# A two-layer hybrid decoder step on one core: a new split of a background job's work between two stages of layer 0

## The chip, the cores and the metric

The kernel runs on one core of a Trainium2 chip. The metric is the device time of one execution in microseconds (us), median of several runs.

## The reference, cut to what matters

One inference step for a prompt group (512 tokens) and a sample group (8 tokens, one for each of 8 batches, with 4096 cached positions each). Both groups use the same weights. Per layer:

```
def layer_forward(x, ...):
    xn = rms_norm(x, norm1_g)
    z, xbc, dt, q, k, v, iq, ik, iw, gate_a, gate_b = split(xn @ w_in)
    y_a = mamba2_branch(...)              # causal conv over xbc, then the state-space scan
    y_b = dsa_prompt(...) or dsa_sample(...)
    x = x + (sigmoid(gate_a) * (y_a @ w_branch_a) + sigmoid(gate_b) * (y_b @ w_branch_b)) @ w_out
    return x + peer_ffn(rms_norm(x, norm2_g))

def dsa_sample(...):                      # the part that is moved here belongs to this
    score = indexer_scores(iq, concat([ik_past, ik]), iw)      # 4097 scores per batch
    _, idx = top_k(score, 256)
    return sparse_attend(q, gathered cache_k rows, gathered cache_v rows)

def peer_ffn(xn):                         # 8 heads x 16 experts for each token
    s = einsum(xn @ wq, keys); sv, si = top_k(s, 16)           # routing
    act = gelu(einsum(u[eidx], xn)); return einsum(gate * act, v[eidx])
```

## The kernel before

The prompt's 512 tokens are cut into two halves of two 128-token tiles, `Half(0)` and `Half(1)`. For each layer and each half the kernel runs through a fixed row of stages: norm1, xbc (projection and causal convolution, `project_conv`), tokproj, ssd, ssmout, qkv, attn0, attn1, mix, norm2, pscore, route. A stage (`stage`, L127) is a block in which each engine has its own in-order stream; at its end all five engines meet at a barrier (L133), so a stage lasts as long as its last engine.

Beside these stages up to three background jobs run. Job "S" (`Sample`) does the decode mixer of the 8 sample tokens; job "U" does the expert dot products (gathered rows of `peer_u` times the token), job "V" the expert sums. A job is a set of generators, one for each engine, that yield a due time in the job's own units before each piece. `PLAN_SAMPLE` (and `PLAN_DOTS`, `PLAN_SUMS`) say how many of the job's units belong to each stage; within a stage, `Beside.to` issues, at points of the stage's own work (`go(part)`), the pieces whose share of the stage's units has come. The order within each engine's stream is thus fixed when the program is built; nothing is scheduled at run time.

Job "S" has 405 units: the state-space part 0 to 80, qkv 80 to 110, the index scores 110 to 165, the top-k 165 to 295, the sparse attention 303 to 405 (`SAMPLE_PARTS`). It begins with the mix stage of half 0 and ends with the tokproj stage of half 1. The end of the top-k is the packing of the keys' positions (the "key packing"): the 129 score columns of two halves of the batches are worked through in 14 chunks, 6 of 19 columns and one of 15 for each half (`sample_topk_vector`, L1874 to L1884). VectorE makes two one-hot tables and a payload in four instructions for each chunk (L1878, L1880, L1882, L1883); TensorE then does one small fp32 matmul a column (L1802, two records each in the trace), waiting with `hot` for VectorE's chunk, and VectorE waits with `taken` so that it is at most two chunks ahead. Then VectorE copies two results (L1888, `packed`), SyncE issues 16 small DMAs to `ssel` and waits for them (L1901 to L1903), and the sparse attention begins: `s_qz` (L1914 to L1918) on VectorE, transposes of `ssel` and the spreading of the new key (L1985, L1990) on TensorE, row numbers (L1924 to L1927), 16 key and value gathers of four batches in a row on GpSimd's queue (L1974), and for each batch a chain that goes back and forth: patch (L1934, VectorE), transposes (L2005, TensorE), copy `s_kT` (L1937, VectorE), scores (L2015, TensorE), scale and maximum (L1941 to L1944, VectorE), exponential (ScalarE), transposes (L2020, TensorE), copy (L1947, VectorE), values (L2025, TensorE), scale (L1953, VectorE).

In the xbc stage of half 1 there are 24 blocks f of 128 channels. TensorE does 16 matmul records for a block (L533), ScalarE evacuates it (L553 to L556), VectorE convolves it in four instructions (L581, L583), ScalarE applies SiLU. Three PSUM banks and two buffers of `raw` and `conv` let TensorE run some blocks ahead of VectorE. Job "U" runs beside it in layer 0: 49 expert rows, each a gather on GpSimd's queue (L2619) into a ring of five rows and one instruction on VectorE (L2655), which frees the row for the next gather. In layer 0 neither "U" nor "V" runs beside the route stage of half 0, since there are no experts yet.

Where a piece falls in a stage follows from the units. A chunk u is due on VectorE at 165 + 130 x (0.63 + 0.025 x (u + 0.2)) and on TensorE at 165 + 130 x (0.63 + 0.025 x (u + 1)).

Of the kernel before, what the change touches and what calls it, by code (L numbers as in the profile page):

```python
# [346 lines left out]
def turn_vectors(nc, G, l, rows, taps, fetch):  # L347

    early = G.ahead.goals()
    with stage(nc, G, "vectors", "vectors") as (block, sem):  # L350
        loaded, goal = (sem("loaded"), 16 * 11) if fetch else (G.ahead.sems[0], early[0])

        if fetch:
            @block.sync
            def _(sp):
                for dst, src in vector_loads(G, l, rows, taps):
                    sp.dma_start(dst, src).then_inc(sem("loaded"), 16)
                sp.wait_ge(sem("loaded"), 16 * 11)

        @block.tensor  # L360
        def _(pe):
            pe.wait_ge(loaded, goal)
            pe.transpose(G.bank[2][:, 0:32], rows[:], G.ident[0:32, 0:32])
            for f in range(FT):
                last = pe.transpose(G.bank[f // 16][:, 32 * (f % 16):32 * (f % 16) + BC_ROWS],
                                    taps[:, f * P:(f + 1) * P], G.ident[0:BC_ROWS, 0:BC_ROWS])
            last.then_inc(sem("turned"), 1)

        @block.vector
        def _(dve):  # L370
            dve.wait_ge(sem("turned"), 1)
            done = Own(dve, sem("copied"))
            done.mark(dve.tensor_copy(G.gcol[:], G.bank[2][:, 0:32]))
            for h in range(2):
                n = min(16, FT - 16 * h)
                src = G.bank[h][:, 0:32 * n].rearrange("p (f c) -> p f c", c=32)[:, :, 0:BC_ROWS]
                done.mark(dve.tensor_copy(G.taps[:, 16 * h:16 * h + n, :], src))

            dve.memset(G.hT[:], 0.0)
            dve.wait_ge(sem("exp"), 1)  # L380
            done(dve.tensor_scalar(G.na[:], G.na[:], -1.0, None, ALU.mult))

        @block.scalar
        def _(act):
            act.wait_ge(loaded, goal)
            act.activation(G.na[:], G.na[:], ACT.Exp).then_inc(sem("exp"), 1)
# [104 lines left out]
def conv_weights(G, l, u):  # L491

    return G.w_in[l, :, C_XBC + 2 * P * u:C_XBC + 2 * P * (u + 1)].rearrange("(k p) c -> p k c", p=P)
# [145 lines left out]
def token_weights(G, l, chunk):  # L639

    return G.w_in[l, :, chunk[0]:chunk[0] + chunk[2]].rearrange("(k p) c -> p k c", p=P)
# [358 lines left out]
def tail_rows(G, S, t):  # L1000

    rows = slice(t * P, t * P + P)
    return (S.tail[:], G.tokm[rows, T_Q:T_Q + QKV]), (S.cs[:], G.rope[rows])
# [375 lines left out]
SAMPLE_TIME = 405.0  # L1379
# [747 lines left out]
SAMPLE = {"POOL": sample_pool, "SP": sample_sync, "DVE": sample_vector, "ACT": sample_scalar, "PE": sample_tensor}  # L2127
# [4 lines left out]
def gate_weights(G, l):  # L2132

    return G.w_in[l, :, C_GA:C_GA + 2 * P].rearrange("(k p) c -> p k c", p=P)
# [664 lines left out]
def hybrid_step(nc, ins, outs, rope):  # L2799
    G = Names()  # L2800
# [19 lines left out]
    with ExitStack() as top:  # L2820
        def sb(name, shape, dt=F32, stack=top):
            return stack.enter_context(nc.sbuf_tensor(name, shape, dt, allow_name_mangling=True))
# [55 lines left out]
        for l in range(DEPTH):  # L2878
            for H in (Half(0), Half(1)):
                with ExitStack() as mixer:  # L2880
                    def keep(name, shape):
                        return mixer.enter_context(nc.sbuf_tensor(name, shape, F32, side="right", allow_name_mangling=True))
                    with ExitStack() as ssm:
                        if not H.late and l == 0:
                            with nc.sbuf_tensor("gain_rows", [32, P], F32, allow_name_mangling=True) as rows, \
                                    nc.sbuf_tensor("tap_rows", [BC_ROWS, CD], F32, allow_name_mangling=True) as taps:
                                turn_vectors(nc, G, l, rows, taps, True)
                        with nc.sbuf_tensor("wx", [P, 4, KD, 2 * P], F32, side="right", allow_name_mangling=True) as wx:
                            wt = wx[:].rearrange("p (s h) k c -> p s (h k c)", h=2).rearrange("p s (k c) -> p s k c", c=BANK)
                            norm_tokens(nc, G, H, 0, "norm1", True, [[(wx[:, u], conv_weights(G, l, u))] for u in range(2)])  # L2890
                            G.xcT = sb("xcT", [P, FT, H.n_in], stack=ssm)
                            project_conv(nc, G, H, l, wx, [(wt[:, 0, :, 0:chunks[0][2]], token_weights(G, l, chunks[0]))], "xbc")
                            project_tokens(nc, G, H, l, chunks, wt, "tokproj")
                        if H.late:
                            G.beside.finish("S")
                            G.stale.append(range(SAMPLE_SEM0, SAMPLE_SEM0 + SAMPLE_SEMS))
                            store_conv_state(nc, G, l, "convst")
                        G.yaT = keep("yaT", [P, XT, H.n_out])
                        if True:
                            S = Names()  # L2900
                            at = Region(nc, f"m{l}{H.i}_", G.region)
                            S.y, S.xs, S.z = at("y", [P, DI]), at("xs", [P, DI]), at("ztile", [P, DI])
                            S.xdd, S.ytmp = at("xdd", [P, 2, DI // NG]), at("ytmp", [P, DI // NG])
                            A = Names()
                            at = Region(nc, f"a{l}{H.i}_", G.region)
                            A.qT, A.iqT, A.roped = at("qT", [P, AH // 2, P]), at("iqT", [P, IH // 2, P]), at("roped", [P, ROPED + 1, HD])
                            at.top = at.base + 2 * 4 * DI
                            A.tail, A.cs = at("tail", [P, QKV]), at("cs", [P, 2, HD // 2])
                            for j, t in enumerate(H.tiles):
                                ssd_chunk(nc, G, S, l, t, j, "ssd")  # L2910
                                ssm_output(nc, G, S, l, P, t * P, j * P, H.late and j == 1, tail_rows(G, A, H.tiles[0]) if j == 1 else (), "ssmout")
                    G.ybT = keep("ybT", [P, KD, H.n_out])
                    wm = keep("wm0", [P, KD, 2 * P])
                    if True:
                        S = A
                        for j, t in enumerate(H.tiles):
                            rows = slice(t * P, (t + 1) * P)
                            attention_inputs(nc, G, S, l, P, t, t * P, j == 0,
                                             (G.k_prompt[l, 0, rows].rearrange("t h d -> t (h d)"),
                                              G.v_prompt[l, 0, rows].rearrange("t h d -> t (h d)"), G.idx_k_prompt[l, 0, rows]), "qkv")  # L2920
                            attention_prompt(nc, G, S, l, t, j, j == 0, [(wm[:], gate_weights(G, l))] if j == 1 else [], f"attn{j}")
                    if not H.late:
                        G.beside.begin("S", Job(SAMPLE, Sample(nc, G, l, G.region), SAMPLE_TIME, PLAN_SAMPLE, ORDER_SAMPLE))
                    G.mixT = keep("mixT", [P, KD, H.n_out])
                    mix_branches(nc, G, H, l, wm, "mix")
                G.g2src = G.norm2_g[l]
                with ExitStack() as peer:
# [5 lines left out]
                    S = Names()  # L2933
# [58 lines left out]
ORDER_FIRST = ("norm1", "xbc", "tokproj", "ssd", "ssmout", "ssd", "ssmout", "qkv", "attn0", "qkv", "attn1", "mix", "norm2", "pscore", "route")  # L2992
ORDER = (("route2", "vectors") + ORDER_FIRST, ORDER_FIRST[:3] + ("convst",) + ORDER_FIRST[3:] + ("route2",))
ORDER_SAMPLE = ("mix", "norm2", "pscore", "route", "norm1", "xbc", "tokproj")
PLAN_SAMPLE = {"mix": 165, "norm2": 4, "pscore": 74, "route": 56, "norm1": 4, "xbc": 32, "tokproj": 70}
PLAN_DOTS = ({"route2": 22, "vectors": 4, "norm1": 0, "xbc": 37, "tokproj": 90, "ssd": 10, "ssmout": 3, "attn0": 14, "attn1": 26, "mix": 54,
              "last": 247, "last_rush": 0.88},
             {"norm1": 0, "xbc": 50, "tokproj": 85, "convst": 5, "ssd": 10, "ssmout": 2, "attn0": 22, "attn1": 24, "mix": 51})
# [46 lines left out]
```

## Time and profile before

| | |
|---|---|
| median of 3 runs | 5554.57 us (5540.15 to 5554.66) |
| profiled execution, its own time | 5553.32 us |
| its span | 5551.6 us |
| TensorE / VectorE / GpSimd / ScalarE busy | 78% / 64% / 45% / 22% of the span |
| mean granted TensorE clock | 0.869 of full speed |

The span is what the profiler saw of the program; 1.7 us of the execution's own time lie around it. No engine is busy throughout; which of them sets the time has to be read stage by stage. The stages spoken of here were located by the barrier's instructions (L133): pscore 822.7 to 896.2, route 896.2 to 1048.1, norm1 1048.1 to 1061.9, xbc 1061.9 to 1204.7, tokproj 1204.7 to 1401.5 us from the span's start.

### The profile page before, as it was taken

How to read it: one execution, taken by the hardware profiler on the slowest of the kernel's cores; microseconds unless marked ns; L12 is line 12 of the kernel's file. 1: busy time of each engine (PE TensorE's matmuls, PEld its weight loads, DVE VectorE, ACT ScalarE, POOL GpSimd, SP SyncE). 2: the span in 40 equal slices, each digit the busy share in tenths (PEclk: the TensorE clock that was granted, in tenths of full speed). 3: DMA queues.
4: the chain of work that ended last, by engine and by line, in shares of the span. 5: the costliest groups of instructions: out<-in, count | busy, mean ns of one | idle time of the engine just before them, and what ended most of it. 6: DMA issues, size and time to landing. Idle time of an engine off the chain costs nothing. (4 is left out here: it accounts for less than half of the span.)

```text
span 5551.6 us, 50287 instructions
## 1 busy us (share of the span) xinstructions
PE 4303.1 (78%) x15868; PEld 2639.8 (48%) x15868; DVE 3538.2 (64%) x7830; ACT 1214.3 (22%) x3036; POOL 2477.7 (45%) x2215
## 2 busy tenths in 40 slices
PE   7955886668678989589677786968778798767777
PEld 6334775543334766263344575553344476223333
DVE  4055648866678546686676868966668754844444
ACT  2042311121332112120432311121233211111111
POOL 0000010166455544546565333456655553577776
PEclk9975997689788999899898898988888899888888
DMA  4310641489788987789889876689878797799999
GB/s 142 117 62 29 236 151 43 150 282 346 261 274 270 328 291 271 276 307 375 289 299 319 322 247 221 204 295 341 300 261 278 269 360 264 258 371 409 409 409 360
DMA packets 583999, 1484.68 MB, mean 267 GB/s; under 512 B 60616, under 2 KB 251688, under 8 KB 581320
## 3 DMA queue, kind: packets, MB, share of 16 engines
q0 software_dynamic: 307200, 1115.82, 55.6%
q1 hardware_dynamic: 261272, 331.39, 18.0%
q10 hardware_dynamic: 15264, 34.26, 1.6%
q8 instruction: 129, 2.11, 0.2%
q14 instruction: 134, 1.10, 0.1%
HBM read 1435.37 MB, written 45.93 MB: 267 GB/s over the span
## 5 line engine op out<-in xcount | busy, mean ns | idle before, releaser
L2747 PE MATMUL duo<-vring,diag 128*128 128x512 f32 (+1 forms) x2976 | 1516.1, 660 | 397.0 <-DMA vring<-in_peer_v,eidx 169.0
L2619 POOL DMA_INDIRECT uring<-in_peer_u,eidx x981 | 1147.4, 1170 | 1117.6 <-DVE uring L2655 661.4
L2700 POOL DMA_INDIRECT vring<-in_peer_v,eidx x1024 | 1127.5, 1101 | 1035.9 <-PE duo L2747 471.8
L2747 PEld LDWEIGHTS duo<-vring,diag 128*128 128x128 f32 (+1 forms) x2976 | 593.9, 209 | 1199.9 <-issue 955.0
L2655 DVE SCALAR_TENSOR_TENSOR uring<-uring,xr 128x1024 f32<-128x1024 f32 x795 | 958.6, 1221 | 200.9 <-DMA uring<-in_peer_u,eidx 177.0
L689 PE MATMUL duo<-wx,xT 128*128 128x512 f32 (+3 forms) x1440 | 607.7, 580 | 32.2 <-PEq L133 32.1
L2780 DVE SCALAR_TENSOR_TENSOR x_tok<-vring,wt,x_tok 128x1024 f32<-128x1024 f32 x296 | 385.3, 1302 | 94.2 <-DMA vring<-in_peer_v,eidx 67.8
L2728 ACT ACTIVATE diag<-ident,wt 128x128 f32<-128x128 f32 x728 | 269.6, 395 | 742.0 <-PE duo L2747 677.9
L689 PEld LDWEIGHTS duo<-wx,xT 128*128 128x128 f32 (+1 forms) x1440 | 240.1, 178 | 387.1 <-issue 386.0
L2655 DVE SCALAR_TENSOR_TENSOR uring<-uring,duo 128x1024 f32<-128x1024 f32 x201 | 245.4, 1221 | 264.5 <-DMA uring<-in_peer_u,eidx 263.9
L533 PE MATMUL duo<-xT,wx 128*128 128x264 f32 (+1 forms) x1536 | 357.5, 397 | 36.6 <-ACT newcols L556 30.3
L533 PEld LDWEIGHTS duo<-xT,wx 128*128 128x128 f32 x1536 | 302.9, 198 | 91.5 <-issue 35.9
L1673 POOL IOTA s_rowi<- 128x8 int32 x2 | 0.3, 148 | 692.3 <-DVEq L1372 692.3
L2215 PE MATMUL duo<-xT,wm 128*128 128x256 f32 (+1 forms) x1024 | 251.2, 405 | 18.2 <-PEq L133 8.8
L2215 PE MATMUL duo<-yaT,wm 128*128 128x256 f32 (+1 forms) x1024 | 250.6, 406 | 16.8 <-DMA wm<-in_w_branch_a 16.5
L2321 PE MATMUL duo<-xT,wq 128*128 128x256 f32 (+1 forms) x1024 | 244.4, 394 | 0.0
L2215 PEld LDWEIGHTS duo<-xT,wm 128*128 128x128 f32 x1024 | 204.9, 202 | 62.2 <-issue 16.3
L2215 PEld LDWEIGHTS duo<-yaT,wm 128*128 128x128 f32 x1024 | 205.7, 203 | 57.9 <-DMA wm<-in_w_branch_a 19.1
L2321 PEld LDWEIGHTS duo<-xT,wq 128*128 128x128 f32 x1024 | 197.7, 198 | 29.3
L1802 PE MATMUL duo<-s_pay,s_hota 128*64 128x32 f32 x1032 | 91.7, 260 | 80.3 <-DVEq L1884 80.3
L1168 PE MATMUL duo<-kT,a_qT 64*128 64x128 f32 (+3 forms) x256 | 103.7, 535 | 58.8 <-DVE s L1264 47.7
L583 DVE SCALAR_TENSOR_TENSOR conv<-raw,taps,conv 128x256 f32<-128x256 f32 x288 | 139.6, 485 | 10.2
(471 smaller groups left out, 5262.4 us busy)
## 6 DMA issues: line engine op xcount, KB each, us to landing
wx<-in_w_in SPq DMA_DIRECT2D x32, 2048.0 KB
wx<-in_w_in SPq DMA_DIRECT2D x48, 1024.0 KB, 8.2
wm<-in_w_in SPq DMA_DIRECT2D x32, 1024.0 KB, 11.4
wm<-in_w_branch_a SPq DMA_DIRECT2D x32, 1024.0 KB, 11.2
wq<-in_peer_wq SPq DMA_DIRECT2D x32, 1024.0 KB, 7.8
tokm<-tout ACTq DMA_DIRECT2D x64, 256.0 KB
eb<-decays SPq DMA_DIRECT2D x32, 512.0 KB, 4.4
s_h<-in_state_ssm SPq DMA_DIRECT2D x32, 512.0 KB, 9.2
```

The lines of the kernel that those rows point to most:

```text
L533: mm = pe.matmul(G.bank[f % NB][:, 0:n], w[:, u % NW, k, (f % 2) * P:(f % 2 + 1) * P], G.xT[:, k, 0:n], start=(k == 0), stop=(k == KD - 1))
L583: last = dve.scalar_tensor_tensor(a, win, tap, a, ALU.mult, ALU.add)
L689: mm = pe.matmul(G.bank[u % 3][0:n, 0:width], G.xT[:, k, j * P:j * P + n], w[:, s, k, 0:width], start=(k == 0), stop=(k == KD - 1))
L1168: mm = pe.matmul(duo[0][:, q, 0:W], S.qT[lo:lo + HD, c, :], G.kT[lo:lo + HD, g // 2, 0:W], start=True, stop=True)
L2215: mm = pe.matmul(tile_bank(c, part, f)[:, 0:n], w[u % NW][:, k, f * P:(f + 1) * P], acts[name][:, k0 + k, 0:n], start=(k0 + k == 0), stop= ...
L2321: mm = pe.matmul(b[:, 0:n], w[:, u % NW, k, (f % 2) * P:(f % 2 + 1) * P], G.xT[:, k, 0:n], start=(k == 0), stop=(k == KD - 1))
L2619: pool.indirect_dma_start(out=E.rings.urows[K % E.ur], out_offset=None, in_=table, in_offset=bass.IndirectOffsetOnAxis(ap=E.tiles[q][3][:, ...
L2655: dve.scalar_tensor_tensor(row, row, 1.0, xr, ALU.mult, ALU.mult, accum_out=G.pre[:, q % 2, j:j + 1]).then_inc(G.dotted, 1)
L2700: pool.indirect_dma_start(out=E.rings.vrows[K % E.vr], out_offset=None, in_=table, in_offset=bass.IndirectOffsetOnAxis(ap=E.tiles[q][3][:, ...
L2728: act.activation(G.diag[:, K % DR, 0:m], sel, ACT.Copy, scale=G.wt[:, q % 2, j:j + 1]).then_inc(G.diagged, 1)
L2747: mm = pe.matmul(G.bank[6 + c][0:m, :], G.diag[:, R % DR, 0:m], E.rings.vrows[K % E.vr][:, c * BANK:(c + 1) * BANK], start=first, stop=las ...
L2780: dve.scalar_tensor_tensor(x, E.rings.vrows[K % E.vr], G.wt[:, q % 2, j:j + 1], x, ALU.mult, ALU.add).then_inc(G.folded, 1)
```

## The change

`PLAN_SAMPLE` becomes a pair, one plan for each layer. Layer 1 keeps the numbers. In layer 0 the route stage of half 0 gets 28 units in place of 56, and the xbc stage of half 1 gets 60 in place of 32; the sum stays 405. The stages' bounds in the job's units move from route 243 to 299, norm1 to 303, xbc to 335 to route 243 to 271, norm1 to 275, xbc to 335.

```
-    G.beside.begin("S", Job(SAMPLE, Sample(nc, G, l, G.region), SAMPLE_TIME, PLAN_SAMPLE, ORDER_SAMPLE))
+    G.beside.begin("S", Job(SAMPLE, Sample(nc, G, l, G.region), SAMPLE_TIME, PLAN_SAMPLE[l], ORDER_SAMPLE))
...
-PLAN_SAMPLE = {"mix": 165, "norm2": 4, "pscore": 74, "route": 56, "norm1": 4, "xbc": 32, "tokproj": 70}
+PLAN_SAMPLE = ({"mix": 165, "norm2": 4, "pscore": 74, "route": 28, "norm1": 4, "xbc": 60, "tokproj": 70},
+               {"mix": 165, "norm2": 4, "pscore": 74, "route": 56, "norm1": 4, "xbc": 32, "tokproj": 70})
```

## Rows read from the trace of the kernel before

**Rows 1.** The page: span, and busy time of each engine.
```profile
span 5551.6 us, 50287 instructions
...
PE 4303.1 (78%) x15868; PEld 2639.8 (48%) x15868; DVE 3538.2 (64%) x7830; ACT 1214.3 (22%) x3036; POOL 2477.7 (45%) x2215
```

**Rows 2.** Windows, route: us, busy PE, PEld, DVE, ACT, POOL, PEclk, DMA share, GB/s.
```profile
896.20:1045.90 149.70, 57.96 (x516) 56.08 (x516) 141.38 (x546) 1.90 (x3) 0.00 (x0) 0.50 0.00 1
1045.90:1048.10 2.20, 0.00 (x0) 0.00 (x0) 0.00 (x0) 0.00 (x0) 0.00 (x0) 0.50 0.02 1
```

**Rows 3.** Windows of the xbc stage, cut where VectorE's stalls begin and end.
```profile
1061.90:1071.70 9.80, 7.40 (x20) 6.02 (x21) 0.02 (x1) 0.54 (x3) 0.00 (x0) 0.56 1.00 323
1071.70:1113.90 42.20, 42.20 (x198) 37.14 (x197) 41.06 (x86) 14.37 (x47) 25.67 (x21) 1.00 0.94 336
1113.90:1131.70 17.80, 8.97 (x42) 7.56 (x40) 1.50 (x5) 0.93 (x4) 13.53 (x15) 0.82 0.89 278
...
1154.30:1204.70 50.40, 37.01 (x138) 27.76 (x138) 38.23 (x80) 15.53 (x39) 23.63 (x20) 0.80 0.68 233
```

**Rows 4.** Timeline of VectorE, route: start us, us, instruction. A full chunk, a narrow one, `packed`.
```profile
957.61 1.42 DVE L1878 TENSOR_TENSOR s_hota<-s_digf,colf 128x1216 f32<-128x1216 f32 x1
...
960.52 2.29 DVE L2450 TENSOR_TENSOR hot<-ab,iota 128x2048 f32<-128x2048 f32 x1
...
1026.86 1.16 DVE L1878 TENSOR_TENSOR s_hota<-s_digf,colf 128x960 f32<-128x960 f32 x1
...
1029.30 2.29 DVE L2450 TENSOR_TENSOR hot<-ab,iota 128x2048 f32<-128x2048 f32 x1
...
1036.27 0.28 DVE L1888 COPY s_packed<-duo 64x32 f32<-64x32 f32 x2
```

**Rows 5.** Timeline of SyncE's queue from the end of route.
```profile
1036.58 10.06 SPq L1901 DMA_DIRECT2D ssel<-s_packed  x16
```

**Rows 6.** Timeline of TensorE: a full chunk's matmuls in layer 0, and in layer 1.
```profile
960.48 4.26 PE L1802 MATMUL duo<-s_pay,s_hota 128*64 128x32 f32 x38 [5.61 <-DVEq L1884]
```
```profile
3483.70 2.40 PE L1802 MATMUL duo<-s_pay,s_hota 128*64 128x32 f32 x38
```

**Rows 7.** Timeline of TensorE and VectorE, norm1 and the start of xbc.
```profile
1059.53 2.05 PE L1990 MATMUL duo<-newkv,ident 8*128 8x256 f32 x4
1064.30 2.08 PE L533 MATMUL duo<-xT,wx 128*128 128x256 f32 x4 [2.72 <-DMA wx<-in_w_in]
```
```profile
1059.28 0.19 DVE L439 TENSOR_TENSOR xT<-duo,gcol 128x32 f32<-128x32 f32 x1 [0.16 <-PE duo L452]
1059.47 0.27 DVE L1914 MEMSET s_qz<- 128x256 f32 x1
1059.78 0.82 DVE L1918 COPY s_qz<-qTs 64x32 f32<-64x32 f32 x4
```

**Rows 8.** Timeline of VectorE, xbc: two successive blocks' convolutions, the stall behind the gathers.
```profile
1075.80 0.35 DVE L581 TENSOR_SCALAR conv<-raw,taps 128x256 f32<-128x256 f32 x1
...
1079.92 0.35 DVE L581 TENSOR_SCALAR conv<-raw,taps 128x256 f32<-128x256 f32 x1
```
```profile
1131.68 1.23 DVE L2655 SCALAR_TENSOR_TENSOR uring<-uring,xr 128x1024 f32<-128x1024 f32 x1 [16.19 <-DMA uring<-in_peer_u,eidx]
```

**Rows 9.** Timeline of TensorE, xbc, while the first batch of the sparse attention runs.
```profile
1155.09 1.12 PE L2005 MATMUL duo<-ident,s_kv 128*128 128x128 f32 x4 [11.38 <-DVE s_kv L1934]
...
1158.13 5.95 PE L533 MATMUL duo<-xT,wx 128*128 128x256 f32 x16
1167.32 1.89 PE L2015 MATMUL duo<-s_kT,s_qz 128*16 128x256 f32 x4 [3.24 <-DVEq L1938]
...
1181.10 0.30 PE L2020 MATMUL duo<-ident,s_s 16*128 16x16 f32 x2 [2.94 <-ACT s_s L2042]
```

**Rows 10.** Timeline of VectorE, xbc: convolutions that waited for TensorE's block.
```profile
1164.69 0.35 DVE L581 TENSOR_SCALAR conv<-raw,taps 128x256 f32<-128x256 f32 x1 [3.20 <-ACT newcols L556]
...
1175.32 0.35 DVE L581 TENSOR_SCALAR conv<-raw,taps 128x256 f32<-128x256 f32 x1 [5.58 <-ACT newcols L556]
```

## The prediction

> **What bounds the kernel now.** I read the page first, for whether one engine fills the span: none does, TensorE is busy for 78% and VectorE for 64% [rows 1], so an edit has to be priced in its own stages. Then I laid windows over route, norm1 and xbc, where work goes out and comes in. In route VectorE has work for 141.4 of the 149.7 us until its last instruction, and the rest lies between its instructions; for 2.2 us more all engines are idle [rows 2]. That stage is one serial VectorE stream and then a wait for SyncE: 16 small DMAs are issued from 1036.58 for 10.06 us, the last issued at 1046.6, and the barrier opens only when they have landed [rows 5]. In xbc nothing is computed on VectorE for 9.8 us, until the first block is projected; then comes a stretch of 42.2 us in which VectorE works for 41.1; then 17.8 us in which it does 1.5 us of work; and at the end 50.4 us with 38.2 busy [rows 3]. The reader is to see that VectorE's order paces this stage, and that its idle time lies in three definite places. The timelines say which: the long stall waits for a gathered expert row [rows 8], and the late ones for blocks that TensorE brings late because it goes back and forth with VectorE over the sparse attention [rows 9, 10].
>
> **What leaves route.** With 28 units for route a chunk is due on VectorE at fraction (165 + 130 x (0.63 + 0.025 x (u + 0.2)) - 243) / 28. Chunk 7 comes to 0.975 and chunk 8 to 1.09. So chunks 8 to 13 leave, one for norm1 and five for xbc. A full chunk holds VectorE from 957.61 to the next instruction at 960.52, 2.91 us; a narrow one from 1026.86 to 1029.30, 2.44 us [rows 4]. Chunk 13 is narrow: 5 x 2.91 + 2.44 = 17.0 us. The `packed` copies leave too: 0.3 us, with the gap behind them 0.4 [rows 4]. Nothing else covers these, as TensorE's matmuls for them (4.26 us each [rows 6]) run beside VectorE's other work. And the 16 DMAs go to xbc, with them the 2.2 us tail [rows 2]. Together -19.5 us (17.4 + 2.1, as the barrier itself stays). This is the firm part.
>
> **norm1.** It gets VectorE's chunk 8 (2.9 us) and TensorE's chunk 7 (38 records at the cold rate, 4.1 us), both behind tile 0. It loses `s_qz` (1.3 us on VectorE) and the spreading (2.05 us and the transposes before it on TensorE) [rows 7]. The three tiles' transposes are behind chunk 7, so VectorE's last `xT` ends some 4.1 us later, at 1063.6 instead of 1059.5, and the barrier comes at about 1063.7 instead of 1061.9: +1.8. But the first matmul of xbc waited for its weights until 1064.30 [rows 7], at a DMA share of 1.00 [rows 3], so the weights hide this. Another effect has the other sign: TensorE then works nearly without a pause from its first transposes into xbc. If that leaves its granted clock at 2.4 GHz, the first 16 records are quicker by up to 16 x (0.427 - 0.216) = 3.4 us (rates: 42.2 us over 198 records at full clock are 0.213 [rows 3], with the gaps 0.216; cold it is twice that). I take 0, with bounds of -3.4 and +1.8.
>
> **xbc, VectorE's own work.** Five chunks, 4 x 2.91 + 2.44 = 14.1; `packed` 0.4; `s_qz` 1.3: 15.8 us. The cover would be idle time of VectorE. Chunks 9 to 13 are due at 0.03, 0.08, 0.14, 0.19 and 0.25, and `packed` at 0.30, so they stand behind blocks 0, 2, 3, 4, 5 and 7. The first 9.8 us of idle time are over by then (chunk 9 stands behind block 0's convolution in VectorE's stream), and behind them comes the stretch that is 97% busy, two rows and a convolution in 4.12 us per block [rows 3, 8]. So the 15.8 us lie on the path in full. Queued behind each chunk are two expert rows and the next convolution, and behind that ScalarE's evacuation and TensorE.
>
> **xbc, TensorE's part.** The six chunks 8 to 13 of matmuls are 5 x 38 + 30 = 220 records, 23.5 us at layer 0's rate (4.1 to 4.26 for 38) and 13.9 at layer 1's (2.40) [rows 6]. A block takes 3.4 us of TensorE against VectorE's 4.12, so some of it fits: per chunk VectorE gains 2.9 and TensorE 2.4. But TensorE's order now has it wait for VectorE's chunk behind block f before block f + 2, where it ran four to five blocks ahead. A VectorE wait of about 2 us should come of that at two places. I take +4, bounds 0 (all hidden) and 13.9.
>
> **xbc, the gathers.** GpSimd issues the 16 key and value gathers in a row, which starves the ring of five rows: 16.19 us [rows 8]. They move from fraction 0.32 to 0.64 of the stage, still one row of 16, still ahead of the same ring. The stall moves and stays: +1, bounds 0 and +2. For SyncE's queue: `ssel` holds it for 10.06 us plus the landing, between the weight loads for u = 7 and u = 8. TensorE wants u = 8 at block 16, VectorE is then past block 11, and the stall behind the gathers comes later. I price it at nothing; without that cover it is 11 us.
>
> **xbc, the back and forth.** This is where I expect the loss. The attention's first batch keeps its order, but the blocks between its steps halve, since 32 units became 60. As blocks behind which each step stands (V for VectorE, T for TensorE):
> before: patch V15, transposes T16, `s_kT` V17, scores T17, scale V18, exponential 19, transposes T19, copy V20, values T21, scale V21;
> after: V19, T19, V20, T20, V21, 21, T21, V22, T22, V22.
> Before, TensorE had done a block more than VectorE when it waited, so VectorE had a convolution to do meanwhile. After, TensorE can't begin block f + 1 until VectorE is done with f and the step; VectorE has only two rows, 2.3 us, to fill with.
> From patch to the next late convolution: TensorE's transposes at 1155.09 to 1164.69, 9.6 us [rows 9, 10], less 2.3: 7.3 idle (before 3.20). `s_kT`, scores from 1167.32 to the convolution at 1175.32, 8.0, with the hand-over before it 8.1, less 2.3: 5.8 (before 5.58); if TensorE is still at 2.4 GHz, 16 x 0.213 + 0.9 + 0.6 less 2.3, 2.6. The scale step: the exponential kept TensorE waiting for 2.94 us [rows 9], of which I count 1.9; 16 records 3.4, evacuation and the rest 1.0, less 2.3: 4.0, and 3.4 more cold. The copy: 1.0 + 3.4 + 0.7 less 2.3: 2.8, and 3.2 more cold. Sum 16.7 to 26.5. Before, the last stretch had 50.4 - 38.2 = 12.2 idle [rows 3]. So +4.5 to +14.3; I take +10, as waits of 3.24 and 11.38 us in rows 9 were followed by cold matmuls and these would be as long.
>
> The Trainium skill ("TensorE: Matmul & The Clock Gate", section "Loop structure matters more than you think") holds that copying results out by VectorE between matmuls does not break the array's warmth, while a long wait does. By it alone the cold parts drop out, the back and forth costs +4.5 and the whole +6. The trace disagrees for a wait of 3.24 us: the row behind it runs 1.89 us for four records.
>
> **Sum.** -19.5 + 0 + 15.8 + 4 + 1 + 10 = +11.3 us. Bounds: -19.5 - 3.4 + 15.8 + 0 + 0 + 4.5 = -2.6, and -19.5 + 1.8 + 15.8 + 13.9 + 2 + 14.3 = +28.3. The profiled execution took 5553.3 (span 5551.6 and 1.7 around it), 1.3 below the median of 5554.6; the change is added to the median: 5565.9. Tokproj has the same pieces in the same order and begins at a barrier, so I carry nothing over.
>
> **Rivals.** First, xbc absorbs it: 5535.1. Its VectorE is idle for some 40 us [rows 3], more than the 15.8 that come. For it: only if chunks ran in that idle time would they be free. Against: they are due in the first third, where idle is 1.1 of 42.2 us. It decides once the stage grows by less than 2.8 us (19.5 less 0.3%, 16.7). With part of it, the result is a gain too. Chance 0.12.
> Second, only VectorE's own work counts, and TensorE keeps its lead: -19.5 + 15.8 = -3.7, 5550.9. Against it: the table of blocks. It ends within 0.3%; I count it with "same".
> Third, the coupling is near its upper bound, TensorE cold through it, perhaps with u = 8 late: +20 to +28, 5580. For it: TensorE waits at every step and has 4.26 us of matmuls for a chunk when cold. Chance 0.33 for all that lies above +16.7.
> That the change does nothing can't be: chunks do change stages.
>
> **Numbers.** 0.3%, 16.7 us, is about what a measurement of this kernel can tell from no change. My forecast of +11 with its neighbours from -16.7 to +16.7, the second rival in it: 0.55. The likeliest one's own range is 5552 to 5583. For 8 in 10 the range takes in the low bound and part of the first rival: 5545 to 5584.
>
> **What would show it.** Route 132 to 133 us, and no idle tail before its barrier. Norm1 about 15.5, and xbc's first matmul near 16.2 us after norm1's start. xbc 170 to 177 in place of 142.8; six chunks' L1802 in it; the 16 us stall once, behind block 17; several waits of 3 to 7 us for `newcols` behind blocks 19 to 22. The prediction is wrong if xbc grows by under 20 us (the coupling or the chunks hide) or by over 36, or if tokproj changes by more than 3.

## The result, and the profile after

The changed kernel takes 5558.4 us (median of 18 runs, 5546.1 to 5568.9), the kernel before 5546.3 us on the same chip (18 runs). The ratio is 1.0024, with a 95% interval of 1.0014 to 1.0033: slower by 13.3 us, 7.8 to 18.3. That is inside the 0.3% that was named as the least a measurement can tell, and these runs did tell it. The forecast was +11.3 us, with 0.55 for "within 0.3%", and 5558.4 lies in the range of 5545 to 5584. The forecast was added to a median of 5554.6 for the kernel before; on this chip that kernel is 8.3 us quicker, so the difference is what to compare: +13.3 against +11.3.

The profiled execution of the changed kernel took 5551.8 us, with this head of its page (the lines that answer to [rows 1]):

```profile
span 5550.0 us, 50279 instructions
...
PE 4298.2 (77%) x15868; PEld 2627.9 (47%) x15868; DVE 3539.8 (64%) x7830; ACT 1213.6 (22%) x3036; POOL 2477.3 (45%) x2215
```

Its span is 1.6 us shorter than the one before, although the medians say 12 us longer. Single executions of either kernel scatter by some 10 us either way, so two spans can't be subtracted here. Lengths of stages can, once one knows how much a stage scatters. For that the kernel before was profiled a second time. Layer 0's stages in us, from the barriers in the traces:

```
                 pscore  route  norm1    xbc  tokproj
before             73.5  151.9   13.8  142.8    196.8
before, again      72.6  151.9   13.8  141.0    190.8
changed            73.3  132.1   16.0  171.4    189.3
difference         -0.2  -19.8   +2.2  +28.6     -7.5
```

(The difference is changed less before.) Route and norm1 repeat to 0.1 us, xbc to 2, tokproj only to 6. So most of tokproj's -7.5 can't be put down to the change: the second profile of the unchanged kernel shows 6.0 of it. An effect of 1 to 3 us isn't excluded: over all profiles of this document tokproj took 190.8 to 196.8 us where the attention keeps its old places in xbc, and 189.3 to 192.5 where it has the new ones. The prediction had named "tokproj changes by more than 3" as a sign of being wrong; the number is met, but a stage that moves by 6 on its own can't serve as such a sign. Route, norm1 and xbc give -19.8 + 2.2 + 28.6 = +11.0 us, inside the measured interval.

Windows over those stages of the changed kernel (us, then busy us and instructions of PE, PEld, DVE, ACT, POOL, then PEclk, DMA share, GB/s):

```profile
895.30:1027.15 131.85, 28.99 (x258) 28.05 (x258) 125.16 (x520) 1.82 (x3) 0.00 (x0) 0.50 0.00 0
...
1027.40:1043.40 16.00, 9.01 (x62) 8.19 (x62) 6.09 (x13) 8.05 (x11) 4.72 (x5) 0.50 0.94 344
1043.40:1050.50 7.10, 6.71 (x28) 5.31 (x28) 0.00 (x0) 0.54 (x3) 0.00 (x0) 0.63 0.98 314
1050.50:1098.00 47.50, 44.53 (x330) 38.28 (x329) 41.90 (x77) 7.94 (x29) 18.98 (x14) 0.89 0.63 205
...
1147.80:1165.70 17.90, 0.00 (x0) 0.00 (x0) 0.03 (x2) 0.00 (x0) 13.64 (x15) 0.59 0.68 230
...
1173.40:1214.80 41.40, 26.14 (x90) 18.49 (x90) 22.18 (x46) 10.31 (x24) 15.81 (x12) 0.83 0.40 136
```

Route lost its 2.2 us tail: VectorE works until 0.25 us before the barrier. The stretch without VectorE at the start of xbc is 7.1 us, not the 9.8 of [rows 3]. The stall with nothing on TensorE and little on VectorE is still 17.9 us long, later in the stage. And the last 41.4 us have only 22.2 busy on VectorE; before, the last 50.4 had 38.2.

What VectorE waited for in the whole xbc stage (us in total, times, longest), first in the kernel before, then in the changed one:

```profile
DVE conv L581 <- ACT newcols L556: 20.9, 4, 11.1
DVE uring L2655 <- DMA uring<-in_peer_u,eidx: 17.0, 2, 16.2
```
```profile
DVE conv L581 <- ACT newcols L556: 30.7, 10, 7.4
DVE uring L2655 <- DMA uring<-in_peer_u,eidx: 18.4, 2, 17.9
```

Waits for the block (`newcols`) rose from 4 to 10 and from 20.9 to 30.7 us; waits for gathered rows rose by 1.4 us only. VectorE's timeline says which ten they are; here are eight of them, and the row behind the gathers:

```profile
1050.51 0.35 DVE L581 TENSOR_SCALAR conv<-raw,taps 128x256 f32<-128x256 f32 x1 [7.37 <-ACT newcols L556]
...
1063.01 0.35 DVE L581 TENSOR_SCALAR conv<-raw,taps 128x256 f32<-128x256 f32 x1 [1.27 <-ACT newcols L556]
...
1097.63 0.35 DVE L581 TENSOR_SCALAR conv<-raw,taps 128x256 f32<-128x256 f32 x1 [1.52 <-ACT newcols L556]
...
1122.13 0.35 DVE L581 TENSOR_SCALAR conv<-raw,taps 128x256 f32<-128x256 f32 x1 [1.88 <-ACT newcols L556]
...
1165.71 1.22 DVE L2655 SCALAR_TENSOR_TENSOR uring<-uring,xr 128x1024 f32<-128x1024 f32 x1 [17.88 <-DMA uring<-in_peer_u,eidx]
...
1183.83 0.35 DVE L581 TENSOR_SCALAR conv<-raw,taps 128x256 f32<-128x256 f32 x1 [7.43 <-ACT newcols L556]
...
1191.76 0.35 DVE L581 TENSOR_SCALAR conv<-raw,taps 128x256 f32<-128x256 f32 x1 [2.88 <-ACT newcols L556]
...
1201.49 0.35 DVE L581 TENSOR_SCALAR conv<-raw,taps 128x256 f32<-128x256 f32 x1 [4.60 <-ACT newcols L556]
...
1208.86 0.35 DVE L581 TENSOR_SCALAR conv<-raw,taps 128x256 f32<-128x256 f32 x1 [2.50 <-ACT newcols L556]
```

They fall into four kinds. The first is the start of the stage. Four short ones (1.27, 1.52 and two not shown of 0.48 and 0.76, 4.0 us together) stand where a packing chunk's matmuls sit before TensorE's next block. One of 1.88 us at 1122 stands alone, behind the step in which TensorE transposes `ssel`. The last four, 7.43 + 2.88 + 4.60 + 2.50 = 17.4 us, stand at the steps of the sparse attention, each behind work that TensorE did for it. TensorE's timeline for these steps and for the wait at 1122 (in brackets what it waited for). "Cold" stands for a granted clock of 0.50, the 1.2 GHz level, and "warm" for 1.00, the 2.4 GHz level:

```profile
1113.12 0.41 PE L1985 MATMUL duo<-ident,ssel 8*128 8x8 f32 x4 [2.28 <-SPq L1372]
1113.39 1.94 PE L1990 MATMUL duo<-newkv,ident 8*128 8x256 f32 x4
...
1174.29 1.09 PE L2005 MATMUL duo<-ident,s_kv 128*128 128x128 f32 x4 [28.64 <-DVE s_kv L1934]
...
1177.31 5.91 PE L533 MATMUL duo<-xT,wx 128*128 128x256 f32 x16
1186.46 1.04 PE L2015 MATMUL duo<-s_kT,s_qz 128*16 128x256 f32 x4 [3.24 <-DVEq L1938]
...
1195.30 0.32 PE L2020 MATMUL duo<-ident,s_s 16*128 16x16 f32 x2 [4.15 <-ACT s_s L2042]
1195.55 5.33 PE L533 MATMUL duo<-xT,wx 128*128 128x256 f32 x16
1203.57 1.04 PE L2025 MATMUL duo<-s_kv,s_pT 128*16 128x256 f32 x4 [2.68 <-DVE s_pT L1947]
1204.53 3.72 PE L533 MATMUL duo<-xT,wx 128*128 128x256 f32 x16
```

The back and forth can be read straight off: TensorE waits for VectorE's step, does the step's matmuls, projects one block of 16 records, and only then VectorE's convolution can run. The row at 1113.12 is the wait that I had priced at nothing. `ssel` is ready only when SyncE's 16 small DMAs have landed, and TensorE stands still for it; what that cost VectorE is weighed further down. SyncE's queue of the changed kernel shows the issue that precedes it, 10.1 us long:

```profile
1099.77 10.10 SPq L1901 DMA_DIRECT2D ssel<-s_packed  x16
...
1113.14 1.01 SPq L515 DMA_DIRECT2D wx<-in_w_in  x2
```

### The profile page after: what moved, and what is told of

The parts are those of the page before. It is cut to its first block and busy times, and to the rows that moved or that the text cites. A ratio compares the mean times of both kernels' runs of the same rounds, so it can differ in the third digit from the quotient of the medians.

```text
span 5550.0 us, 50279 instructions
## 1 busy us (share of the span) xinstructions
PE 4298.2 (77%) x15868; PEld 2627.9 (47%) x15868; DVE 3539.8 (64%) x7830; ACT 1213.6 (22%) x3036; POOL 2477.3 (45%) x2215
## 3 DMA queue, kind: packets, MB, share of 16 engines
q8 instruction: 129, 2.11, 0.2%
## 5 line engine op out<-in xcount | busy, mean ns | idle before, releaser
L2655 DVE SCALAR_TENSOR_TENSOR uring<-uring,xr 128x1024 f32<-128x1024 f32 x795 | 959.1, 1221 | 206.9 <-DMA uring<-in_peer_u,eidx 181.6
L2655 DVE SCALAR_TENSOR_TENSOR uring<-uring,duo 128x1024 f32<-128x1024 f32 x201 | 245.4, 1221 | 265.0 <-DMA uring<-in_peer_u,eidx 264.5
L533 PE MATMUL duo<-xT,wx 128*128 128x264 f32 (+1 forms) x1536 | 365.1, 402 | 20.1 <-ACT newcols L556 16.5
L2215 PE MATMUL duo<-yaT,wm 128*128 128x256 f32 (+1 forms) x1024 | 245.6, 400 | 14.6 <-DMA wm<-in_w_branch_a 14.4
L2215 PEld LDWEIGHTS duo<-xT,wm 128*128 128x128 f32 x1024 | 203.7, 201 | 62.3 <-issue 16.9
L2215 PEld LDWEIGHTS duo<-yaT,wm 128*128 128x128 f32 x1024 | 202.2, 199 | 54.2 <-DMA wm<-in_w_branch_a 16.9
L2321 PEld LDWEIGHTS duo<-xT,wq 128*128 128x128 f32 x1024 | 196.8, 197 | 28.9
## 6 DMA issues: line engine op xcount, KB each, us to landing
wm<-in_w_in SPq DMA_DIRECT2D x32, 1024.0 KB, 11.3
```

Source lines behind the costliest of these rows:

```text
L533: mm = pe.matmul(G.bank[f % NB][:, 0:n], w[:, u % NW, k, (f % 2) * P:(f % 2 + 1) * P], G.xT[:, k, 0:n], start=(k == 0), stop=(k == KD - 1))
L2215: mm = pe.matmul(tile_bank(c, part, f)[:, 0:n], w[u % NW][:, k, f * P:(f + 1) * P], acts[name][:, k0 + k, 0:n], start=(k0 + k == 0), stop= ...
L2321: mm = pe.matmul(b[:, 0:n], w[:, u % NW, k, (f % 2) * P:(f % 2 + 1) * P], G.xT[:, k, 0:n], start=(k == 0), stop=(k == KD - 1))
L2655: dve.scalar_tensor_tensor(row, row, 1.0, xr, ALU.mult, ALU.mult, accum_out=G.pre[:, q % 2, j:j + 1]).then_inc(G.dotted, 1)
```

## The experiments

The two theories at the start. Mine: xbc pays for VectorE's own work in full, and then for an attention in which TensorE no longer runs ahead of VectorE, because its steps are spread over half as many blocks each. The rival: the chunks alone cost (their work, their matmuls, the place of the stall), and the attention's new spacing costs nothing. One experiment moves the attention alone, one the chunks alone. Line numbers of the experiments' kernels are shifted where lines were added (L2655 is L2657 or L2670).

**The kernel before, once more** (`before_again`), unchanged.

> The kernel before, unchanged, for one more profile: how much its stages vary from execution to execution, above all tokproj of half 1 in layer 0, which took 196.8 us in the first profile and 189.3 in the changed kernel's. If that stage's length is chance, this profile has it anywhere from 188 to 198 us, while route (151.9) and xbc (142.8) repeat within 1 us. If the shorter tokproj belongs to the change, this profile shows 196 to 198 again.

It took 5547.6 us. The table above has its stages: route and norm1 equal, xbc 1.8 us shorter (more than the 1 us that I had allowed), tokproj 6.0 us shorter.

**The attention alone** (`attend_only`): the kernel before and its plan, but layer 0's steps that were due between 303 and 335 units are due between 317.9 and 335, where the changed kernel has them. The chunks stay in route.

```diff
+MOVE = ((303.0, 303.0 + 32.0 * 28 / 60), (335.0, 335.0))
...
+def at_moved(program):
+    def steps(eng, J):
+        for t in program(eng, J):
+            yield moved(t) if J.l == 0 else t
+    return steps
...
```

The function `moved`, left out here, is linear between the points of `MOVE`; `at_moved` wraps every engine's part of job "S".

> The kernel before with its plan, and in layer 0 only the sparse attention's pieces at the places of the stage that the change gives them (due times 303 to 335 squeezed into 317.9 to 335); the key packing stays beside routing. My theory, that the back and forth loses TensorE's lead: route stays at 151.9 us, norm1 gets some 0.5 us shorter, xbc grows by the 1.3 us of s_qz and by 5 to 14 us of waits for blocks, 149 to 157 us in place of 142.8; in all 5 to 13 us slower, 1.001 to 1.0023. The rival, that only VectorE's own work counts: xbc 144 us, time unchanged. The stall behind the gathers stays at 16 us and moves to block 17.

Ratio 1.0028 (1.0014 to 1.0042), so +15.5 us. Norm1 took 11.6 us (-2.2), xbc 159.7 (+16.9); together +14.7. VectorE's waits in its xbc, and the four late convolutions:

```profile
DVE conv L581 <- ACT newcols L556: 33.1, 5, 11.7
DVE uring L2670 <- DMA uring<-in_peer_u,eidx: 18.3, 4, 16.6
```
```profile
1177.47 0.35 DVE L581 TENSOR_SCALAR conv<-raw,taps 128x256 f32<-128x256 f32 x1 [7.83 <-ACT newcols L556]
...
1188.28 0.35 DVE L581 TENSOR_SCALAR conv<-raw,taps 128x256 f32<-128x256 f32 x1 [5.76 <-ACT newcols L556]
...
1198.07 0.35 DVE L581 TENSOR_SCALAR conv<-raw,taps 128x256 f32<-128x256 f32 x1 [4.65 <-ACT newcols L556]
...
1206.85 0.35 DVE L581 TENSOR_SCALAR conv<-raw,taps 128x256 f32<-128x256 f32 x1 [3.17 <-ACT newcols L556]
```

The late ones sum to 21.4 us, against 9.85 in the kernel before (3.20 and 5.58 [rows 10] and one of 1.07). So with not a single chunk moved, the respacing of the attention alone makes the kernel slower by about as much as the whole change does (1.0028 and 1.0024, with intervals that overlap), and 11.6 of the 14.7 us are in these waits. The rival, which gave 0 here, is refuted; my own 149 to 157 for xbc was too low, by 3.

The ten profiles of this document bear it out. The waits of VectorE for a block in the attention's part of xbc sum to 7.3 to 9.9 us in the six in which the attention stands at about its old places, and to 17.3 to 21.4 us in the four in which it stands at the new ones.

**The chunks alone** (`chunks_only`): the changed kernel, with layer 0's attention steps pulled back to about the blocks that they stood behind before.

```diff
+MOVE = ((303.0, 303.0), (313.2, 306.8), (323.4, 313.25), (335.0, 335.0))
```

The functions around it are those of `attend_only`.

> The changed kernel, but with the sparse attention's first batches at the places of the xbc stage that they had before (patch at 0.64 of the stage in place of 0.81; the gathers at 0.53, as they have to come behind the packing). My theory: route 132 us as in the changed kernel, xbc shorter than the changed kernel's 171.4 by 5 to 12 us, 159 to 166 us, as the waits behind blocks 19 to 22 fall from 17 to 6 to 12 us; against the kernel before -2 to +6 us in all, ratio 0.9995 to 1.001. The rival (only VectorE's own work and the packing's matmuls cost, not the spacing of the attention): xbc stays at 170 to 172 us and the ratio at 1.0024.

Ratio 0.9992 (0.9978 to 1.0007): no difference that can be told. Route (132.2) and norm1 (16.0) are as in the changed kernel; xbc 159.2, 12.2 us less than it. VectorE's waits:

```profile
DVE conv L581 <- ACT newcols L556: 20.9, 7, 7.5
DVE uring L2670 <- DMA uring<-in_peer_u,eidx: 14.5, 1, 14.5
DVE s_kv L1934 <- DMA s_kv<-in_cache_v,s_coli: 1.5, 1, 1.5
```

Against the changed kernel that is 9.8 less for `newcols`, 3.9 less for gathered rows and 1.5 more for `s_kv`: the 12.2 us, to the tenth. The chunks by themselves cost xbc 16.4 us and earn 19.7 - 2.2 in route and norm1: 1 us is left over, less than these profiles can tell. VectorE's busy time in xbc is 102.1 us in the kernel before and 117.0 here, its idle time 40.7 and 42.1: the work that came found no cover. Other changes cancel in that idle time, as the stage starts sooner and the waits for gathers are shorter, while the chunks bring short waits of their own, one of them 3.7 us.

The two parts taken singly add 16.4 and 16.9 to xbc, 33.3 together, and 28.6 when both are made, so 4.7 us are counted twice. `s_qz`, 1.3 us, moves into xbc in both. The first convolution, seen from the stage's start, comes 1.6 us later in `attend_only` and 2.6 sooner in `chunks_only`, but 2.7 sooner with both, which is 1.8 more. The late waits give 1.8 again (+11.6, -2.3, and +7.6 with both). The other waits nearly cancel.

**The gathers spread** (`spread_before`, `spread_after`). The 16 us stall [rows 8] didn't go away and grew by 1.7 us at most. I had put it down to 16 gathers that GpSimd issues in a row. The test puts places for the ring's rows between them, in the kernel before and in the changed one (both layers).

```diff
     for b in range(DECB):
+        if 0 < b < KV_RING:
+            yield at(0.1 + 0.06 * b)
         if b >= KV_RING:
```

> The kernel before, with the 16 key and value gathers of the first four batches no longer issued in one row but four for each batch, at 0.10, 0.16, 0.22 and 0.28 of the attention (both layers). My theory, that the 16.2 us stall is the ring of five expert rows starved by one row of 16 gathers: the stall falls to under 3 us, xbc of layer 0 to some 127 us, and layer 1 gains what such a stall costs there, 0 to 16 us; in all 12 to 32 us faster, ratio 0.994 to 0.998. The rival, that the transfers themselves (the DMA engines are busy for 0.89 of that stretch) and not the order on GpSimd's queue set it: xbc stays at 138 to 143 us.

Ratio 0.9959 (0.9945 to 0.9974), -22.7 us. Layer 0's xbc 128.9 us (-13.9), layer 1's 128.8 after 139.5 (-10.7), 24.6 together. VectorE's waits in layer 0's xbc:

```profile
DVE conv L581 <- ACT newcols L556: 16.6, 4, 9.3
DVE uring L2657 <- DMA uring<-in_peer_u,eidx: 7.1, 4, 4.6
```

The wait for gathered rows fell from 17.0 to 7.1 us although the same gathers are issued, so 10 us of it were the order on GpSimd's queue; the rival's 138 to 143 us for xbc is refuted. I had expected under 3 us, and what holds the other 7.1 was not tried. The waits for blocks are 4.3 us shorter as well; between the two profiles of the kernel before they differ by 1.9.

> The changed kernel with the gathers of the first four batches spread as in spread_before (both layers). If the change's loss is independent of the stall behind the gathers, as I hold, this kernel stands to spread_before as the changed kernel to the one before: 0.9959 + 0.0024 = 0.998, xbc 128.9 + 28 = 155 to 158 us. The rival (the stall of 18 us and the back and forth share a cause, so that without the stall TensorE has still less lead and the loss grows): xbc over 162 us, ratio over 1.000.

Ratio to the kernel before 0.9973 (0.9963 to 0.9984); xbc 161.2 us, expected 155 to 158.

```profile
DVE conv L581 <- ACT newcols L556: 31.3, 8, 7.1
DVE uring L2657 <- DMA uring<-in_peer_u,eidx: 6.3, 3, 5.6
```

Most of the stall is gone here too (6.3 left of 18.4), and `newcols` stays at 31.3. In the profiles the change costs xbc 161.2 - 128.9 = 32.3 us without the stall and 28.6 with it, which misses my range towards the rival's. The runs lean the other way: the two ratios differ by 0.0014, less than the 0.0024 of the change, with intervals that overlap. So nothing shows that stall and loss depend on each other, and one profile each can't exclude some 4 us. What stands is that the loss is there without the stall: it is not a loss to the gathers.

**TensorE's chunks a block later** (`late_matmuls`): the changed kernel, with the due time of each chunk's matmuls in layer 0 moved by 0.9 of a step, so that VectorE is well past the chunk when TensorE comes to it.

```diff
-        yield at(0.63 + 0.35 * (u + 1) / len(chunks))
+        yield at(min(0.98, 0.63 + 0.35 * (u + (1.9 if J.l == 0 else 1)) / len(chunks)))
```

> The changed kernel with the packing's matmuls in layer 0 due 0.9 of a chunk later on TensorE, so that TensorE is a block further on when it waits for VectorE's chunk. My theory, that the four waits of the convolution in the packing's part of xbc (1.27, 0.48, 0.76 and 1.52 us) come of TensorE's lead being cut to one block: they fall to under 1.5 us in all, xbc 167 to 169.5 in place of 171.4. The rival, that they come of the 2.4 us which each chunk's matmuls take on TensorE: the waits stay at 3 to 5 us and xbc at 171 to 172. Norm1 changes by some us too, as chunk 7's matmuls go to another place. The ratio can hardly tell: 1.0017 to 1.0027.

Ratio 1.0026 (1.0017 to 1.0036), norm1 13.8, xbc 173.3, together 0.3 us less than the changed kernel. TensorE's timeline in its xbc, a middle chunk and the last:

```profile
1068.40 2.40 PE L1802 MATMUL duo<-s_pay,s_hota 128*64 128x32 f32 x38
...
1087.25 3.41 PE L1802 MATMUL duo<-s_pay,s_hota 128*64 128x32 f32 x30 [4.49 <-DVEq L1884]
```

The small waits shrank to one of 0.73 us, as meant. But the cap at 0.98 let the last two chunks' matmuls fall behind the same block, TensorE then waited 4.49 us for VectorE, and VectorE 4.99 us for its block. Neither theory had that: xbc is above both ranges, and the run does not decide whether the 4.0 us of short waits could be saved.

**Another stage for other chunks** (`into_pscore`, `spread_into_pscore`): the kernel before with layer 0's plan changed the other way, the first four of route's chunks and the small instructions before them into pscore ahead of it, xbc left alone; and the same with the gathers spread.

```diff
+PLAN_SAMPLE = ({"mix": 165, "norm2": 4, "pscore": 90, "route": 40, "norm1": 4, "xbc": 32, "tokproj": 70},
+               {"mix": 165, "norm2": 4, "pscore": 74, "route": 56, "norm1": 4, "xbc": 32, "tokproj": 70})
```

> The kernel before with 16 of layer 0's 56 route units given to the stage ahead of it, pscore, in place of xbc: 90 and 40. Four chunks and some 2.6 us of small instructions leave route: route 151.9 - 14.2 = 137.7 us. In pscore VectorE has work for 56.3 of 73.5 us, so its added 14.2 us fit into its idle time; TensorE, busy for 68.2, gets three chunks' matmuls, 7.2 us. My theory, that moved work costs what it adds to the engine that paces the receiving stage: pscore 81 to 84 us, in all 3 to 7 us faster, ratio 0.9987 to 0.9995. The rival, that work on any busy engine adds its whole time: pscore 88 us, no gain.

Ratio 0.9989 (0.9978 to 1.0000), 5538.3 us. Route took 137.7 us (-14.2), as expected; pscore 85.7 (+12.2), more than the 81 to 84 expected and less than the rival's 88. TensorE's timeline at the end of its pscore, three chunks' matmuls:

```profile
897.73 2.40 PE L1802 MATMUL duo<-s_pay,s_hota 128*64 128x32 f32 x38 [1.40 <-DVEq L1884]
...
901.07 8.32 PE L1802 MATMUL duo<-s_pay,s_hota 128*64 128x32 f32 x76
```

The pieces stand at the end of the stage, one behind the other, and two of the three chunks' matmuls run at the cold rate: 10.7 us in place of my 7.2. VectorE had 17.2 us of idle time in this stage before and has 16.1 now, so its 13.2 us of new work found 1.1 us of cover: idle time elsewhere in the stage did not help it.

> Both in one: the gathers spread over the first four batches in both layers, and 16 units of layer 0's route given to pscore, xbc and norm1 with the plan of before. If the two are independent: 0.9959 with 3 to 7 us less, ratio 0.9946 to 0.9954; the fastest of these kernels. If they aren't, it stays at 0.996.

Ratio 0.9957 (0.9943 to 0.9972), 5516.9 us, xbc 131.2: the fastest of all by its median, but not told apart from `spread_before` (0.9959), and short of the 0.9946 to 0.9954 expected if the two gains add.

## Why the prediction held, step by step

**What leaves route: -19.5, measured -19.8.** Counting six chunks out, the copies of `packed` and the 2.2 us tail gave the stage to 0.3 us. Every instruction there lies on one serial stream.

**Norm1 and the start: 0 with -3.4 to +1.8, measured -0.5.** Norm1 grew by 2.2 us; the first convolution of xbc came 2.7 us sooner in its stage. Both effects that I set against each other were there. The clock row in norm1 stays at 0.50, and in the first 7.1 us of xbc it is 0.63: the clock rose during the first 16 records, not before them, so most of the 3.4 us was not had. Some 2 of the 2.7 us came from the weights, which TensorE waited for less long (0.88 us, before 2.72 [rows 7]).

**VectorE's own work in xbc: +15.8 on the path in full, measured +16.5.** Its busy time rose from 102.1 to 117.2 us, and the gaps of under 0.3 us between its instructions by 1.3. `chunks_only` shows that nothing covers it: with the attention at about its old places xbc grew by 16.4 us, and VectorE's idle time didn't shrink. The first rival (absorbed by idle time) is refuted by that; the stage as a whole grew by 28.6, and that rival needed under 2.8.

**TensorE's part: +4, measured 4.0** in four short waits. I had expected it as about 2 us at two places; it came as 0.5 to 1.5 at four. In `chunks_only` and `spread_after` the same places have 5.4 and 5.3 us, so the exact hit is luck. (The 23.5 us for 220 cold records should read 23.7 to 24.7; nothing was built on it.) The six chunks' matmuls held TensorE for 14.6 us, five of them for 2.40 us or less each (layer 1's rate in [rows 6]), and most of that fitted beside VectorE's chunks.

**The gathers: +1, measured +1.4; the stall once, 17.9 us, later.** Right, and spreading the gathers shows its cause.

**SyncE's queue: 0, measured +1.9 in the changed kernel's profile and 0 to 0.3 in three others.** I looked at what is queued behind the 16 DMAs, the weight loads, and they did no harm: VectorE never waited for the loads at 1113.14. I didn't look at who waits for their data. In the kernel before the barrier took that wait (the 2.2 us tail that I credited to route); after the change it is TensorE's, 2.28 us before `ssel` is transposed, and VectorE waits 1.88 us for the block behind it. But the wait for `ssel` alone doesn't cost that much. TensorE has it in every kernel in which the packing stands in xbc; here are `chunks_only` and then `spread_after`:

```profile
1116.36 0.41 PE L1985 MATMUL duo<-ident,ssel 8*128 8x8 f32 x4 [2.39 <-SPq L1372]
1116.64 1.10 PE L1990 MATMUL duo<-newkv,ident 8*128 8x256 f32 x4
```
```profile
1117.81 0.41 PE L1987 MATMUL duo<-ident,ssel 8*128 8x8 f32 x4 [2.19 <-SPq L1372]
```

VectorE's wait for the block behind it is 0.34 us in `chunks_only`, and none shows in `spread_after` or in `late_matmuls` (TensorE waits 2.11 us there). What differs is how long TensorE is cold afterwards. Windows of the changed kernel and of `chunks_only`, the granted clock third from the end:

```profile
1113.52:1120.33 6.81, 6.81 (x17) 5.00 (x17) 6.34 (x17) 0.00 (x0) 3.62 (x3) 0.50 0.92 310
```
```profile
1118.61:1122.01 3.40, 3.40 (x9) 2.71 (x9) 3.20 (x10) 0.00 (x0) 1.97 (x3) 0.50 1.01 339
```

It was 6.8 us against 3.4, which is 1.7 us of lost work, and the rows of L1990 show the same (1.94 against 1.10 us). So the tail was moved, and mostly saved, because TensorE still has a lead over VectorE where it now waits; the 0 was priced without looking at this consumer, and held in three kernels of four.

**The back and forth: +10, measured +7.6.** 17.4 us in four waits, against 9.85 before (and 8.5 in its second profile, which would make it +8.9). My single values were 7.3, 2.6 to 5.8, 4.0 to 7.4, 2.8 to 6.0; measured 7.43, 2.88, 4.60, 2.50. So each wait came near its lower end, and the sum of 16.7 to 26.5 at 17.4. The mechanism stands by `attend_only`. The mis-sized part is the cold clock: my +10 stood for 22.2 us of waits, 4.8 too many, as I took most of them to be followed by cold matmuls, and only two of the four blocks behind the steps were partly cold (5.91 and 5.33 us for 16 records), the others took 3.72. The baseline was a second, smaller error of the other sign: I took all 12.2 us of idle time in the last stretch as such waits, and they were 9.85.

The terms measured: -19.8 - 0.5 + 16.5 + 4.0 + 1.4 + 1.9 + 7.6 = +11.1, and the stages give +11.0, the runs +13.3 (7.8 to 18.3). That the sum of +11.3 came out this close is in part luck: +1.9 that I didn't have and -2.4 that I had too much nearly cancel, and xbc by itself moves by 2 us from profile to profile. The second rival (only VectorE's own work, -3.7) and the third (+20 to +28) are both outside the interval; the third's premise, TensorE cold through it, wasn't met.

The Trainium skill ("TensorE: Matmul & The Clock Gate", section "Loop structure matters more than you think") says that VectorE's copying between matmuls doesn't break the warmth and a long wait does. The prediction set this trace's 3.24 us wait followed by cold records against it. In the changed kernel the same wait of 3.24 us is followed by four records in 1.04 us, so it stayed warm. The four waits together, 17.4 us, came close to the 16.7 that this rule gave and far from my 22.2; the growth, +7.6, lies between its +4.5 and my +10, as both were taken from too large a baseline. `attend_only` has both waits again with the cold outcome (last section), so neither the rule nor my reading of it is a law for waits of this length.

## What to carry to other kernels

When background work moves to another stage, its instructions are the easy part of the price: they cost in the new stage what they saved in the old one unless they land in time that is really idle there, and here `chunks_only` came out at zero. The dear part is that a plan by shares respaces everything else in that stage: ask how many blocks each engine may run ahead between two steps of a dialogue, before and after. And when the producer of a wait at the end of a stage moves, find its next consumer: the wait goes there, and is saved only as far as that engine has a lead. Here TensorE waited 2.1 to 2.4 us in four kernels, and VectorE lost 1.9, 0.3 and twice nothing. The larger gain lay in the same rows all the time: 16 gathers in a row on one queue starved another ring for 16 us, and three places between them, in each layer, gave back 22.7 us.

## What the runs showed of the hardware

Equal waits left TensorE at different clocks, even in two executions of one kernel. TensorE's timeline of `attend_only`, to be set beside 1186.46 and 1203.57 of the changed kernel above, and then that of `before_again`, to be set beside 1167.32 of [rows 9]:

```profile
1180.10 1.89 PE L2015 MATMUL duo<-s_kT,s_qz 128*16 128x256 f32 x4 [3.24 <-DVEq L1938]
...
1200.14 1.89 PE L2025 MATMUL duo<-s_kv,s_pT 128*16 128x256 f32 x4 [2.68 <-DVE s_pT L1947]
```
```profile
1164.66 1.04 PE L2015 MATMUL duo<-s_kT,s_qz 128*16 128x256 f32 x4 [3.24 <-DVEq L1938]
```

After a wait of 3.24 us four records take 1.89 us in `attend_only` and in [rows 9] (the 1.2 GHz level), and 1.04 us in the changed kernel and in `before_again` (2.4 GHz). After 2.68 us it is 1.89 in `attend_only` and 1.04 in the changed kernel. The length of the last wait doesn't decide, and neither does the program, since [rows 9] and `before_again` are the same one, with the same instructions before the wait; what else does was not tried. For a forecast it means that such a step has two prices: VectorE's wait behind that row is 5.58 us in the kernel before and 2.88 in its repeat, 5.76 in `attend_only` and 2.88 in the changed kernel. A single profile shows only one of them.
